# Block 2's mixer: the recurrences, convolutions and head norms laid between the weight tiles of its input projection

## The chip, the cores and the metric

The kernel runs on one core of one Trainium2 chip. The metric is the device time of one execution in microseconds, median of several. TensorE multiplies into eight PSUM banks; VectorE, ScalarE and GpSimd (POOL) do the rest; SyncE (SP) issues most DMAs. Each engine runs its own instructions in order and waits on semaphores.

## The reference

Three blocks in a row work on one sequence of 256 tokens with 1024 channels, all in float32. The change lies in the mixer of the second block; a helper that it edits is used in the first block too. Block 2's mixer is, cut to its operations:

```
z = rmsnorm(x) @ w_in                       # 256 x 3072
a_u, a_gate, b_q, b_f, b_v, b_g, c_b, c_c, c_v = split(z)
y_a = RG-LRU:  u = causal conv(a_u, 4 taps); gates r, i = sigmoid(u @ block-diagonal w)
               a linear recurrence over tokens with decay exp(-8 softplus(lambda) r),
               times gelu(a_gate)
y_b = HGRN2:   f = lower bound + (1 - lower bound) sigmoid(b_f); k = 1 - f; q = silu(b_q)
               gated linear attention with decays f over 6 heads of 64, times silu(b_g)
y_c = short convolution of 3 taps over c_b, c_c, c_v products
x = x + concat(y_a, y_b, y_c, each normed per head of 64 with a gain) @ w_out
```

## The kernel before

**Weights.** A matrix is read in tiles of 1 MB through a ring of three slots (`unit`, `split_act`, `split_dve`). ScalarE rounds a tile into its upper part (`hi`), VectorE subtracts for the lower part (`lo`); three pairs of these exist (NP = 3), so the upper split of tile t waits until TensorE is done with tile t-3. A tile of the input projection (8 x 128 rows, 256 columns) is multiplied in 48 matmuls of 256 columns (`unit_mm`): hi with the upper and the lower part of the activations (L430), lo with the upper part (L435).

**Banks.** `Plan.bank` gives out the eight PSUM banks in turn. Whoever takes a bank waits until the one who had it before, eight takings ago, has been read out.

**Block 2's mixer** is four functions on each engine, each with a `meet` at its end, at which every engine waits for all the others:

1. `block2_in`: norm and transposition, then the twelve tiles of `w_in_2` in their own order; VectorE and ScalarE take turns to copy a finished bank to `z` (24 chunks of 128 channels).
2. `rglru`: a chain of small operations on three columns (L2161 to L2183), three convolutions of four taps (`conv_dve`), six gate products on TensorE (L2131), Tanh on ScalarE, the scan (L2204), Sqrt and Gelu.
3. `hgrn`: the forget gate (Exp, L2253 reciprocal, Ln), SiLU of q, three prefix sums (L752), then the decay of nine levels (`decay_dve`, `decay_act`, `decay_pe`). In level li, VectorE computes the difference E (L762), ScalarE takes Abs and Exp of it (L789, L791), VectorE multiplies it into q and k (L766, L767), TensorE computes the scores of six heads into six banks (L814), and VectorE copies them under a mask into `hS` (L781, L778) one level later. Then TensorE computes the outputs.
4. `mix2_out`: short convolution, squares of all eight chunks, their sums over heads (L671), one Sqrt, one reciprocal over 2048 columns (L680), gain and gate, the parts for TensorE (L390, L397), and the four tiles of the output projection (`rows_pe`, L638).

The order within an engine is the order of the Python calls; nothing plans it. In block 1 `decay_*` runs for GLA with two heads' worth of chunks, and a callable `tick` puts modulation tiles between its levels.

Of the kernel before, what the change touches and what calls it, by code (L numbers as in the profile page):

```python
# [2078 lines left out]
Z_TOK = (12, 13, 14)  # L2079


def block2_in_pe(k, e):
# [2 lines left out]
    first_units_pe(k, e, [k.bank(e, "w_in_2", g) for g in range(2)], u0, ((), ()), "mix2", t["a2_hi"], t["a2_lo"])
    for g in range(2, 12):
        unit_mm(k, e, k.bank(e, "w_in_2", g), u0 + g, t["a2_hi"], t["a2_lo"], [j for j in range(2) if 2 * g + j in Z_TOK])
    meet(k, e, PE_, "z")
# [20 lines left out]

def block2_in_dve(k, e):  # L2110
    t = k.t
# [4 lines left out]
    for g in range(12):  # L2116
        u = k.first["w_in_2"] + g
        split_dve(k, e, u + 3)
        if g % 2 == 0:
            e.wait_ge(*k.used(u))  # L2120
            e.tensor_copy(flat(pair(t["z"], g)), k.got("w_in_2", g)[:, :]).then_inc(*k.DVE(frees=("w_in_2", g)))
    meet(k, e, DVE_, "z")


def rglru_pe(k, e):
    t = k.t
    e.wait_ge(*k.total("rg_in"))
    e.wait_ge(*k.dve("rg", "u"))
    for n, bd, o, _ in RG:
        for c in range(3):  # L2130
            e.matmul(k.bank(e, "rg", o, c)[:, 0:256], t[bd][:, c, :], t["u"][:, c, :]).then_inc(*k.MM("rg", o, c))  # L2131
    meet(k, e, PE_, "rg")
# [1500 lines left out]
```

## Time and profile before

| | |
|---|---|
| median of 3 runs (lowest, highest) | 3101.34 us (3097.02, 3104.08) |
| the profiled execution, its span | 3097.4 us, 3095.5 us |
| TensorE busy | 2799.4 us, 90% |
| VectorE, ScalarE, POOL busy | 46%, 30%, 7% |
| mean granted TensorE clock | 0.938 |

All times in the views are microseconds from the first instruction. The granted clock is in parts of full speed, 1.00 for 2.4 GHz and 0.50 for 1.2 GHz; a value between them is a stretch with both.

### The profile page before, as it was taken

The numbers are of one execution on the slowest core, as the hardware profiler recorded it, in microseconds if no ns is written. First come the engines' busy times: TensorE is split into PE (matmuls) and PEld (weight loads), VectorE is DVE, ScalarE is ACT, GpSimd is POOL, SyncE is SP. The second block draws the span as 40 slices with busy tenths as digits, with TensorE's granted clock in tenths as the row PEclk, the third lists the DMA queues.
The fourth block names the chain that finished last, engine by engine and source line by source line (L and its number), as shares of the span: only waits on it lengthen the run. The fifth ranks groups of instructions, "written<-read, shape, count | busy, mean of one in ns | idle before, by whom it ended". The sixth has DMA issues, their size and how long they took to land. (4 is left out here: it accounts for less than half of the span.)

```text
span 3095.5 us, 42024 instructions
## 1 busy us (share of the span) xinstructions
PE 2799.4 (90%) x17693; PEld 2015.5 (65%) x17693; DVE 1423.2 (46%) x2005; ACT 923.8 (30%) x1217; POOL 222.5 (7%) x160
## 2 busy tenths in 40 slices
...
DMA packets 305130, 713.78 MB, mean 231 GB/s; under 512 B 15723, under 2 KB 214073, under 8 KB 271846
## 3 DMA queue, kind: packets, MB, share of 16 engines
...
## 5 line engine op out<-in xcount | busy, mean ns | idle before, releaser
L369 DVE TENSOR_TENSOR lo<-ring,hi 128x2048 fp32r<-128x2048 f32 x251 | 598.5, 2390 | 298.3 <-ACT hi L360 298.3
L360 ACT ACTIVATE hi<-ring 128x2048 fp32r<-128x2048 f32 x251 | 475.5, 1898 | 191.6 <-PE bank L638 131.4
L1721 PE MATMUL bank<-expert,xg 128*64 128x512 f32 x2304 | 523.6, 599 | 0.0
L430 PE MATMUL bank<-x_hi,hi 128*128 128x256 f32 x1568 | 382.8, 284 | 0.0
L430 PE MATMUL bank<-x_lo,hi 128*128 128x256 f32 x1568 | 380.3, 281 | 0.0
L1721 PEld LDWEIGHTS bank<-expert,xg 128*64 128x64 f32 x2304 | 157.8, 137 | 312.4 <-issue 311.2
L430 PEld LDWEIGHTS bank<-x_hi,hi 128*128 128x128 f32 x1568 | 295.0, 188 | 3.3 <-issue 1.6
L430 PEld LDWEIGHTS bank<-x_lo,hi 128*128 128x128 f32 x1568 | 295.5, 188 | 2.5 <-issue 1.0
L1818 DVE TENSOR_TENSOR acc<-bank,acc 128x512 f32<-128x512 f32 x144 | 89.5, 684 | 407.4 <-PE bank L1808 407.3
L1791 PE MATMUL bank<-expert,aT 128*64 128x512 f32 x1152 | 254.9, 595 | 0.9 <-DMA expert<-in_w_mlp 0.9
L1746 DVE TENSOR_SCALAR sx<-bank 128x256 f32<-128x256 f32 x72 | 30.2, 420 | 395.8 <-PE bank L1732 395.2
L435 PE MATMUL bank<-x_hi,lo 128*128 128x256 f32 x1568 | 204.0, 282 | 0.0
L435 PEld LDWEIGHTS bank<-x_hi,lo 128*128 128x128 f32 x1568 | 194.8, 188 | 0.0
L1791 PEld LDWEIGHTS bank<-expert,aT 128*64 128x64 f32 x1152 | 79.6, 137 | 173.9 <-issue 169.8
L1684 PEld LDWEIGHTS bank<-P,htok 128*128 128x128 f32 x1152 | 137.8, 200 | 26.3 <-issue 26.3
L1700 ACT ACTIVATE xg<-bank 128x512 f32<-128x512 f32 x36 | 21.5, 597 | 444.0 <-PE bank L1684 444.0
L638 PE MATMUL bank<-hi,act_hi 128*128 128x512 f32 x448 | 144.5, 396 | 0.0
L638 PE MATMUL bank<-hi,act_lo 128*128 128x512 f32 x448 | 144.4, 396 | 0.0
L1684 PE MATMUL bank<-P,htok 128*128 128x64 f32 x1152 | 142.3, 284 | 1.1 <-DVE P L1615 1.1
L638 PE MATMUL bank<-lo,act_hi 128*128 128x512 f32 x448 | 119.7, 396 | 0.0
L390 ACT ACTIVATE act_hi<-tmp 128x512 fp32r<-128x512 f32 x56 | 35.4, 633 | 253.9 <-DVE tmp L2687 189.5
L736 POOL MEMSET hS<- 128x2304 f32 x1 | 2.0, 2017 | 1385.2 <-DVE unit L2207 1385.2
...
## 6 DMA issues: line engine op xcount, KB each, us to landing
expert<-in_w_mlp SPq DMA_DIRECT2D x384, 1024.0 KB, 11.5
...
```

Of the source, the lines that this page charges most:

```text
L360: e.activation(k.half("hi", u), k.slot(j), ACT.Copy).then_inc(*k.up("hi_done"))
L369: e.tensor_tensor(k.half("lo", u), k.slot(k.units[u][0]), k.half("hi", u).bitcast(F32), SUB).then_inc(*k.up("lo_done"))
L390: e.activation(hi[:, c:n, :], x[:, c:n, :], ACT.Copy).then_inc(*k.ACT(nm, "hi", c // step))
L430: e.matmul(o, l, r, start=fresh, stop=False, skip_group_check=True)
L435: t = e.matmul(o, l, r, start=False, stop=False, skip_group_check=True)
L638: m = e.matmul(acc[b, h][:, :], x[:, c, b * 128:(b + 1) * 128], w[:, c, h * 512:(h + 1) * 512], start=fresh[b, h], stop=False, skip_group_ ...
L1684: m = e.matmul(bank[:, d * CAP:(d + 1) * CAP], t["htok"][:, b, d * 128:(d + 1) * 128], t[f"P{n % 3}"][:, b, :], start=b == 0, stop=b == 1)
L1700: e.activation(flat(k.t[f"xg{n % 3}"]), k.got("xg", n)[:, :], ACT.Copy).then_inc(*k.ACT("xg", n, frees=("xg", n)))
L1721: i = e.matmul(banks[n][j][h * CAP:(h + 1) * CAP, :], x, W[:, (2 * h + j) * 512:(2 * h + j + 1) * 512], start=c == 0, stop=False, skip_gro ...
L1746: e.tensor_scalar(t[f"sx{j}"], bank[:, 0:512:2], 7.0, None, MIN).then_inc(*k.DVE("gate", "x", n, j))
L1791: q = e.matmul(banks[n][h * CAP:(h + 1) * CAP, :], a, W[:, r, h * 512:(h + 1) * 512], start=i + r == 0, stop=i + r == 4, skip_group_check= ...
L1818: e.tensor_tensor(av, k.got("back", n, b, h)[:, :], av, ADD).then_inc(*k.DVE(frees=("back", n, b, h)))
```

## The change

Block 2's four functions on each engine become one (`block2_pe`, `block2_act`, `block2_dve`) without `meet` between them. The tiles of the input projection come in another order (`Z_ORDER`): first those that hold the forget gate and q, then a_u and the rest. Five are multiplied ahead of the decay; `between_pe`, `between_act` and `between_dve` are called in each level and put one of the other seven tiles, its splits and copies, and pieces of RG-LRU and of the short convolution into levels 0 to 6. ScalarE copies every finished bank to `z`. In `decay_dve` and `decay_act` the difference E of level li+1 is computed and exponentiated in level li. The head norms are split by group and done chunk by chunk: those of RG-LRU and of the short convolution after the last level and ahead of HGRN2's; the output projection takes its tiles in the order 0, 3, 1, 2. POOL clears `hS` and the padded tiles before the projection, not after RG-LRU. Most temporaries share space with `z`, `y2` and `sq2`, so `rgg`, `hg`, `xn2` and `a2o_*` go. The lines taken out of the old functions stand above; of the diff the core:

```diff
     e.wait_ge(*k.dve())
     for li in range(10):
+        if li < 8:
+            h = LEVELS[li + 1]
+            nb, r, v = decay_views(k, nm, n, h)
+            P, E = v(k.t[f"{nm}P{r}"]), v(k.t[f"{nm}E{(li + 1) % 2}"])
+            e.wait_ge(*k.dve())
+            e.tensor_tensor(E, P, P[:, :, h - 1:h].to_broadcast([128, nb, 2 * h]), SUB).then_inc(*k.DVE(nm, "E", li + 1))
         if 0 < li < 9:
             h, i = LEVELS[li], li % 2
             nb, r, v = decay_views(k, nm, n, h)
-            P, E = v(k.t[f"{nm}P{r}"]), v(k.t[f"{nm}E{i}"])
+            E = v(k.t[f"{nm}E{i}"])
             if li >= 2:
                 e.wait_ge(*k.mm(nm, "put", li - 2))
-                e.wait_ge(*k.dve())
-            e.tensor_tensor(E, P, P[:, :, h - 1:h].to_broadcast([128, nb, 2 * h]), SUB).then_inc(*k.DVE(nm, "E", li))
             e.wait_ge(*k.pool(nm, f"qe{i}"))
             e.wait_ge(*k.pool(nm, f"ke{i}"))
             e.wait_ge(*k.act(nm, "E", li))
             e.tensor_tensor(v(k.t[f"{nm}qe{i}"])[:, :, h:2 * h], v(flat(q))[:, :, h:2 * h], E[:, :, h:2 * h], MUL).then_inc(*k.DVE())
             e.tensor_tensor(v(k.t[f"{nm}ke{i}"])[:, :, 0:h], v(flat(kk))[:, :, 0:h], E[:, :, 0:h], MUL).then_inc(*k.DVE(nm, "level", li))
+        if between and li < 9:
+            between(k, e, li)
         if li > 0:
...
-def decay_act(k, e, nm, tick=None):
-    for li in range(10):
-        if 0 < li < 9:
-            E = k.t[f"{nm}E{li % 2}"]
-            e.wait_ge(*k.dve(nm, "E", li))
+def decay_act(k, e, nm, between=None):
+    for li in range(9):
+        if li < 8:
+            E = k.t[f"{nm}E{(li + 1) % 2}"]
+            e.wait_ge(*k.dve(nm, "E", li + 1))
             e.activation(E, E, ACT.Abs).then_inc(*k.ACT())
             e.wait_ge(*k.act())
-            e.activation(E, E, ACT.Exp, scale=-1.0).then_inc(*k.ACT(nm, "E", li))
-        if li > 0 and tick:
-            tick(2 if li - 1 < 6 else 0)
...
+def decay_pe(k, e, nm, q, kk, n, between=None):
     for li, h in enumerate(LEVELS):
-        if tick:
-            tick(2 if li < 6 else 0)
...
+MIX_ORDER = (0, 3, 1, 2)
+def z_unit_pe(k, e, n):
+    t, g = k.t, Z_ORDER[n]
+    unit_mm(k, e, k.bank(e, "w_in_2", n), k.first["w_in_2"] + n, t["a2_hi"], t["a2_lo"], [j for j in range(2) if 2 * g + j in Z_TOK])
+def z_unit_act(k, e, n):
+    u = k.first["w_in_2"] + n
+    split_act(k, e, u + 3)
+    e.wait_ge(*k.used(u))
+    e.activation(flat(pair(k.t["z"], Z_ORDER[n])), k.got("w_in_2", n)[:, :], ACT.Copy).then_inc(*k.ACT("z", n, frees=("w_in_2", n)))
+def z_unit_dve(k, e, n):
+    split_dve(k, e, k.first["w_in_2"] + n + 3)
...
+def head_norm_act(k, e, nm, rt):
+    e.wait_ge(*k.dve(nm, "ms"))
+    e.activation(rt, rt, ACT.Sqrt).then_inc(*k.ACT(nm, "rt"))
+def head_sums_dve(k, e, nm, chunks, rt):
+    for i, c in enumerate(chunks):
+        e.wait_ge(*k.mm(nm, c))
+        e.tensor_scalar(rt[:, i, :], k.got(nm, c)[:, 0:256], EPS, None, ADD).then_inc(*k.DVE(frees=(nm, c)))
+    k.mark("dve_done", nm, "ms")
...
+def block2_pe(k, e):
+    t = k.t
+    first_units_pe(k, e, [k.bank(e, "w_in_2", n) for n in range(2)], k.first["w_in_2"], ((), ()), "mix2", t["a2_hi"], t["a2_lo"])
+    for n in (2, 3, 4):
+        z_unit_pe(k, e, n)
+    e.wait_ge(*k.dve("hg", "in"))
+    decay_pe(k, e, "hg", t["hq"], t["hk"], 3, between_pe)
+    head_norm_pe(k, e, "rgn", (0, 1, 2))
+    head_norm_pe(k, e, "scn", (6, 7))
+    e.wait_ge(*k.act("z", 11))
+    e.wait_ge(*k.dve("hg", "score", 8, 2, 1))
+    for c in range(3):
+        bank = k.bank(e, "hg", "out", c)
+        for par in range(2):
+            decay_out(k, e, t["hS"], 2 * c + par, lambda b, o=par * 64, c=c: t["z"][:, 12 + c, b * 128 + o:b * 128 + o + 64],
+                      bank[par * 64:par * 64 + 64, 0:256], *(("hg", "out", c) if par else ()))
+    head_norm_pe(k, e, "hgn", (3, 4, 5))
+    acc = acc_banks(k, e, "w_out_2")
+    for n, i in enumerate(MIX_ORDER):
+        e.wait_ge(*k.dve("y2", "lo", i))
+        rows_pe(k, e, "w_out_2", acc, k.first["w_out_2"] + n, pair(t["a2_hi"], i), pair(t["a2_lo"], i), n == 0, n == 3)
+    acc_free(k, "w_out_2")
+    meet(k, e, PE_, "mix2")
+def between_pe(k, e, li):
+    t = k.t
+    if li == 2:
+        e.wait_ge(*k.total("rg_in"))
+        e.wait_ge(*k.dve("rg", "u"))
+        for n, bd, o, _ in RG:
+            for c in range(3):
+                e.matmul(k.bank(e, "rg", o, c)[:, 0:256], t[bd][:, c, :], t["u"][:, c, :]).then_inc(*k.MM("rg", o, c))
+    if li < 7:
+        z_unit_pe(k, e, 5 + li)
...
+    e1, e0 = t["rg_sm"][:, 3:6], t["hg_sm"][:, 0:3]
+    split_act(k, e, k.first["w_in_2"] + 3)
+    e.activation(e1, k.V["rg_lambda_2"], ACT.Abs).then_inc(*k.ACT())
+    e.wait_ge(*k.act())
+    e.activation(e1, e1, ACT.Exp, scale=-1.0).then_inc(*k.ACT("rg", "e1"))
+    e.wait_ge(*k.dve("hg", "e0"))
+    e.activation(e0, e0, ACT.Exp).then_inc(*k.ACT("hg", "e0"))
+    z_unit_act(k, e, 0)
+    z_unit_act(k, e, 1)
+    e.wait_ge(*k.act())
+    e.activation(f, f, ACT.Exp, scale=-1.0).then_inc(*k.ACT("hg", "f"))
+    z_unit_act(k, e, 2)
+    e.wait_ge(*k.act())
+    e.wait_ge(*k.dve("mix2", "lo", 3))
+    e.activation(t["hth"], t["hq"], ACT.Tanh, scale=0.5).then_inc(*k.ACT("hg", "q"))
+    e.wait_ge(*k.dve("hg", "k"))
+    e.activation(f, f, ACT.Ln).then_inc(*k.ACT("hg", "ln"))
+    z_unit_act(k, e, 3)
+    z_unit_act(k, e, 4)
+    decay_act(k, e, "hg", between_act)
+    for c in range(3):
+        e.wait_ge(*k.mm("hg", "out", c))
+        e.activation(t["y2"][:, 3 + c, :], k.got("hg", "out", c)[:, 0:256], ACT.Copy).then_inc(*k.ACT(frees=("hg", "out", c)))
+    e.wait_ge(*k.act())
+    e.wait_ge(*k.dve("hg", "g"))
+    e.activation(t["sq2"][:, 3:6, :], t["y2"][:, 3:6, :], ACT.Square).then_inc(*k.ACT("hgn", "sq"))
+    mix_upper_act(k, e, 0)
+    mix_upper_act(k, e, 3)
+    head_norm_act(k, e, "hgn", f)
+    u = k.first["w_out_2"]
+    split_act(k, e, u + 3)
+    mix_upper_act(k, e, 1)
+    mix_upper_act(k, e, 2)
+    for n in (1, 2, 3):
+        split_act(k, e, u + n + 3)
+    meet(k, e, ACT_, "mix2")
...
+def between_act(k, e, li):
+    t, sm = k.t, k.t["rg_sm"]
+    if li < 7:
+        z_unit_act(k, e, 5 + li)
+    if li == 2:
+        e.wait_ge(*k.dve("rg", "hb"))
+        for n, bd, o, hb in RG:
+            for c in range(3):
+                e.wait_ge(*k.mm("rg", o, c))
+                e.activation(t[o][:, c, :], k.got("rg", o, c)[:, 0:256], ACT.Tanh, bias=sm[:, hb + c:hb + c + 1], scale=0.5) \
+                    .then_inc(*k.ACT(*(("rg", o) if c == 2 else ()), frees=("rg", o, c)))
+    elif li == 3:
+        e.wait_ge(*k.dve("rg", "log_a"))
+        e.activation(t["a"], t["r"], ACT.Exp).then_inc(*k.ACT("rg", "a"))
+        e.wait_ge(*k.act())
+        e.activation(t["r"], t["r"], ACT.Tanh).then_inc(*k.ACT("rg", "t"))
+    elif li == 4:
+        e.wait_ge(*k.dve("rg", "b2"))
+        e.activation(t["rb2"], t["rb2"], ACT.Sqrt, scale=-1.0).then_inc(*k.ACT("rg", "beta"))
+        e.activation(t["z"][:, 3:6, :], t["z"][:, 3:6, :], ACT.Gelu_apprx_tanh).then_inc(*k.ACT("rg", "gelu"))
+    elif li == 6:
+        e.activation(t["gth"], t["z"][:, 15:18, :], ACT.Tanh, scale=0.5).then_inc(*k.ACT("hg", "g"))
+        e.wait_ge(*k.dve("sc", "y"))
+        e.activation(t["sq2"][:, 6:8, :], t["y2"][:, 6:8, :], ACT.Square).then_inc(*k.ACT("scn", "sq"))
+        e.wait_ge(*k.dve("rg", "y"))
+        e.activation(t["sq2"][:, 0:3, :], t["y2"][:, 0:3, :], ACT.Square).then_inc(*k.ACT("rgn", "sq"))
+    elif li == 8:
+        head_norm_act(k, e, "rgn", t["z"][:, 0:3, :])
+        head_norm_act(k, e, "scn", t["z"][:, 22:24, :])
...
+def block2_dve(k, e):
+    t, sm, hl, f = k.t, k.t["hg_sm"], k.V["hg_lower_bounds_2"], k.t["z"][:, 9:12, :]
+    e0, lb, om = sm[:, 0:3], sm[:, 3:6], sm[:, 6:9]
+    e.tensor_tensor(e0, hl, hl, SUB).then_inc(*k.DVE("hg", "e0"))
+    split_dve(k, e, k.first["w_in_2"] + 3)
+    rg_decay_dve(k, e)
+    e.wait_ge(*k.act("hg", "e0"))
+    e.reciprocal(lb, e0).then_inc(*k.DVE())
+    e.wait_ge(*k.dve())
+    e.tensor_tensor(e0, e0, lb, MUL).then_inc(*k.DVE())
+    e.wait_ge(*k.dve())
+    e.tensor_tensor(lb, e0, e0, SUB).then_inc(*k.DVE())
+    e.wait_ge(*k.dve())
+    e.tensor_scalar(om, lb, -1.0, 1.0, MUL, ADD).then_inc(*k.DVE())
+    z_unit_dve(k, e, 1)
+    e.wait_ge(*k.act("hg", "f"))
+    e.tensor_scalar(f, f, 1.0, None, ADD).then_inc(*k.DVE())
+    z_unit_dve(k, e, 2)
+    e.wait_ge(*k.dve())
+    e.reciprocal(f, f).then_inc(*k.DVE())
+    e.wait_ge(*k.dve())
+    e.tensor_tensor(f, f, along(om, T), MUL).then_inc(*k.DVE())
+    e.wait_ge(*k.dve())
+    e.tensor_tensor(f, f, along(lb, T), ADD).then_inc(*k.DVE())
+    e.wait_ge(*k.dve())
+    e.tensor_scalar(t["hk"], f, -1.0, 1.0, MUL, ADD).then_inc(*k.DVE("hg", "k"))
+    z_unit_dve(k, e, 3)
+    e.wait_ge(*k.act("hg", "q"))
+    silu_dve(k, e, t["hq"], t["hq"], t["hth"], 0.125)
+    k.mark("dve_done", "hg", "in")
+    z_unit_dve(k, e, 4)
+    e.wait_ge(*k.act("hg", "ln"))
+    e.wait_ge(*k.dve())
+    decay_dve(k, e, "hg", t["hq"], t["hk"], f, 3, t["hS"], between_dve)
+    head_sums_dve(k, e, "rgn", (0, 1, 2), t["z"][:, 0:3, :])
+    head_sums_dve(k, e, "scn", (6, 7), t["z"][:, 22:24, :])
+    head_norm_dve(k, e, "rgn", (0, 1, 2), t["z"][:, 0:3, :])
+    head_norm_dve(k, e, "scn", (6, 7), t["z"][:, 22:24, :])
+    mix_lower_dve(k, e, 0)
+    mix_lower_dve(k, e, 3)
+    head_sums_dve(k, e, "hgn", (3, 4, 5), f)
+    e.wait_ge(*k.act("hgn", "sq"))
+    e.tensor_tensor(t["y2"][:, 3:6, :], t["y2"][:, 3:6, :], t["z"][:, 15:18, :], MUL).then_inc(*k.DVE())
+    u = k.first["w_out_2"]
+    split_dve(k, e, u + 3)
+    head_norm_dve(k, e, "hgn", (3, 4, 5), f)
+    mix_lower_dve(k, e, 1)
+    mix_lower_dve(k, e, 2)
+    for n in (1, 2, 3):
+        split_dve(k, e, u + n + 3)
+    meet(k, e, DVE_, "mix2")
...
+def between_dve(k, e, li):
+    t, V, z, y = k.t, k.V, k.t["z"], k.t["y2"]
+    if li < 7:
+        z_unit_dve(k, e, 5 + li)
+    if li == 0:
+        e.wait_ge(*k.act("z", 4))
+        cw = V["rg_conv_w_2"]
+        for c in range(3):
+            conv_dve(k, e, t["u"][:, c, :], z[:, c, :], [cw[:, j * 3 + c:j * 3 + c + 1] for j in range(4)], V["rg_conv_b_2"][:, c:c + 1])
+        k.mark("dve_done", "rg", "u")
+    elif li == 3:
+        for n, bd, o, _ in RG:
+            e.wait_ge(*k.act("rg", o))
+            e.tensor_scalar(t[o], t[o], 0.5, 0.5, MUL, ADD).then_inc(*k.DVE())
+        e.wait_ge(*k.dve())
+        e.tensor_tensor(t["r"], t["r"], along(t["rg_sm"][:, 21:24], T), MUL).then_inc(*k.DVE("rg", "log_a"))
+        e.tensor_tensor(t["ig"], t["ig"], t["u"], MUL).then_inc(*k.DVE())
+    elif li == 4:
+        e.wait_ge(*k.act("rg", "a"))
+        e.tensor_tensor(t["rb2"], t["a"], t["a"], MUL).then_inc(*k.DVE())
+        e.wait_ge(*k.act("rg", "t"))
+        e.wait_ge(*k.dve())
+        e.scalar_tensor_tensor(t["rb2"], t["rb2"], 1.0, t["r"], ADD, MUL).then_inc(*k.DVE("rg", "b2"))
+    elif li == 5:
+        sw = V["sc_conv_w_2"]
+        e.wait_ge(*k.act("z", 8))
+        e.tensor_tensor(z[:, 20:22, :], z[:, 20:22, :], z[:, 22:24, :], MUL).then_inc(*k.DVE())
+        e.wait_ge(*k.dve())
+        for c in range(2):
+            conv_dve(k, e, y[:, 6 + c, :], z[:, 20 + c, :], [sw[:, j * 2 + c:j * 2 + c + 1] for j in range(3)], None)
+        e.wait_ge(*k.dve())
+        e.tensor_tensor(y[:, 6:8, :], y[:, 6:8, :], z[:, 18:20, :], MUL).then_inc(*k.DVE("sc", "y"))
+    elif li == 6:
+        e.wait_ge(*k.act("rg", "beta"))
+        e.tensor_tensor(t["ig"], t["ig"], t["rb2"], MUL).then_inc(*k.DVE())
+        e.wait_ge(*k.dve())
+        for c in range(3):
+            e.tensor_tensor_scan(t["u"][:, c, :], t["a"][:, c, :], t["ig"][:, c, :], 0.0, MUL, ADD).then_inc(*k.DVE())
+        e.wait_ge(*k.act("rg", "gelu"))
+        e.wait_ge(*k.dve())
+        e.tensor_tensor(y[:, 0:3, :], t["u"], z[:, 3:6, :], MUL).then_inc(*k.DVE("rg", "y"))
+    elif li == 7:
+        e.wait_ge(*k.act("hg", "g"))
+        silu_dve(k, e, z[:, 15:18, :], z[:, 15:18, :], t["gth"], 1.0)
+        k.mark("dve_done", "hg", "g")
...
+        z = k.sb("z", [128, 24, 256], F32, c3)
+        k.sb("a2_hi", [128, KC, 256], F32R, c3), k.sb("a2_lo", [128, KC, 256], F32R, c3)
+        k.sb("rg_sm", [128, 24], F32, c3), k.sb("hg_sm", [128, 16], F32, c3)
+        k.sb("hk", [128, 3, 256], F32, c3)
+        k.sb("hS", [128, 6, 3, 128], F32, c3)
+        lay_decay(k, "hg", 3, c3)
+        k.t["hq"], k.t["rb2"] = z[:, 6:9, :], z[:, 0:3, :]
+        k.t["hth"] = k.t["u"] = k.t["sq2"][:, 0:3, :]
+        k.t["r"] = k.t["gth"] = k.t["sq2"][:, 3:6, :]
+        k.t["a"], k.t["ig"] = k.t["y2"][:, 0:3, :], k.t["y2"][:, 3:6, :]
+    for g in Z_ORDER:
+        k.unit("w_in_2", wview(A["w_in_2"][0])[:, :, g * 256:(g + 1) * 256], 8, 256)
+    for i in MIX_ORDER:
+        k.unit("w_out_2", wview(A["w_out_2"][0])[:, 2 * i:2 * i + 2, :], 2, DM)
```

`u + 3` in `z_unit_act` means that the upper split for tile n+2 is issued ahead of the copy of tile n. `rg_decay_dve` holds the small operations that were L2161 to L2183.

## Rows read from the trace of the kernel before

**Rows 1.** Table of stretches (start:end, length, busy by engine, granted clock, DMA share, GB/s)
```profile
1417.70:1477.80 60.10, 59.48 (x504) 59.28 (x503) 26.98 (x16) 22.16 (x16) 0.00 (x0) 1.00 0.55 178
1477.80:1519.70 41.90, 4.46 (x12) 3.39 (x12) 28.43 (x62) 16.88 (x23) 5.15 (x5) 0.57 0.05 21
1519.70:1574.20 54.50, 26.88 (x205) 24.27 (x205) 38.18 (x81) 14.32 (x17) 0.00 (x0) 0.50 0.00 1
1574.20:1616.50 42.30, 10.83 (x44) 6.53 (x44) 28.80 (x23) 6.66 (x6) 0.00 (x0) 0.58 0.00 0
1616.50:1640.70 24.20, 24.15 (x96) 19.11 (x96) 10.77 (x7) 8.18 (x6) 0.00 (x0) 0.93 0.42 132
```

**Rows 2.** Waits of TensorE from 1519.7 to 1640: total, times, longest
```profile
PE bank L814 <- DVE hq L718: 25.1, 1, 25.1
```

**Rows 3.** Timeline of ScalarE, block 2: start, length, operation, idle before
```profile
1477.22 0.60 ACT L2106 ACTIVATE z<-bank 128x512 f32<-128x512 f32 x1 [3.79 <-PE bank L435]
...
1505.19 1.28 ACT L2227 ACT_TABLE_LOAD   x1 [2.28 <-DVE hg_sm L2241]
...
1550.97 0.84 ACT L791 ACTIVATE hgE<-hgE 128x768 f32<-128x768 f32 x1
...
1624.00 1.92 ACT L360 ACTIVATE hi<-ring 128x2048 fp32r<-128x2048 f32 x1 [5.07 <-PE bank L638]
```

**Rows 4.** Timeline of VectorE, block 2
```profile
1508.08 4.95 DVE L2253 RECIPROCAL z<-z 128x768 f32<-128x768 f32 x1
...
1519.74 5.05 DVE L752 TENSOR_TENSOR_SCAN hgP<-early,hg 128x768 f32<-128x768 f32 x3
...
1549.10 0.96 DVE L762 TENSOR_TENSOR hgE<-hgP 128x768 f32<-128x768 f32 x1
...
1552.42 0.55 DVE L767 TENSOR_TENSOR hgke<-hk,hgE 128x384 f32<-128x384 f32 x1
1552.89 2.09 DVE L781 COPY_PREDICATED hS<-im,bank 128x256 f32<-128x256 int32 x6
...
1572.83 1.27 DVE L778 COPY hS<-bank 128x128 f32<-128x128 f32 x6
...
1596.31 12.95 DVE L680 RECIPROCAL xn<-xn 128x2048 f32<-128x2048 f32 x1 [1.98 <-ACT xn L665]
...
1618.96 2.29 DVE L369 TENSOR_TENSOR lo<-ring,hi 128x2048 fp32r<-128x2048 f32 x1 [0.86 <-ACT hi L360]
```

**Rows 5.** Table of stretches, VectorE alone: convolution, RG-LRU, SiLU, short convolution
```profile
1484.30:1490.10 5.80, 5.42 (x13) 0.50 0.00 0
1493.70:1504.80 11.10, 8.64 (x11) 0.65 0.00 0
1579.10:1580.90 1.80, 1.53 (x4) 1.00 0.00 0
1580.90:1585.10 4.20, 3.93 (x8) 0.67 0.00 0
```

**Rows 6.** Timeline of TensorE: first tile, pitch of tiles, gates, scores of a level
```profile
1404.49 3.75 PE L606 MATMUL bank<-a_hi,hi 128*128 128x256 f32 x16 [11.59 <-ACT hi L360]
...
1421.29 2.04 PE L435 MATMUL bank<-a_hi,lo 128*128 128x256 f32 x16
...
1426.92 2.04 PE L435 MATMUL bank<-a_hi,lo 128*128 128x256 f32 x16
...
1490.29 4.46 PE L2131 MATMUL bank<-u,BD 128*128 128x256 f32 x12 [13.11 <-DVE u L729]
...
1541.07 3.09 PE L814 MATMUL bank<-hgqe,hgke 64*128 64x128 f32 x24 [2.89 <-DVE hgke L767]
```

**Rows 7.** Table of stretches, block 1's decay
```profile
148.00:152.00 4.00, 2.88 (x22) 1.69 (x22) 0.76 (x2) 1.03 (x3) 0.00 (x0) 0.59 1.10 353
```

**Rows 8.** Timeline of TensorE, block 1's last two decay levels
```profile
168.35 1.51 PE L814 MATMUL bank<-glaqe,glake 64*128 64x128 f32 x16 [3.09 <-DVE glake L767]
172.70 1.22 PE L810 MATMUL bank<-glaqe,glake 64*128 64x128 f32 x8 [2.85 <-DVE glake L767]
```

More of the change, by code:

```diff
@@ L745, in decay_views, with decay_dve @@
     return W // (2 * h), r, v
-def decay_dve(k, e, nm, q, kk, g, n, S, tick=None):
+def decay_dve(k, e, nm, q, kk, g, n, S, between=None):
     W = n * 256
@@ L2076 @@
 RG = (("rg_w_r_2", "BD0", "r", 15), ("rg_w_i_2", "BD1", "ig", 18))
+Z_ORDER = (4, 5, 3, 0, 1, 2, 9, 10, 11, 8, 7, 6)
 Z_TOK = (12, 13, 14)
-def block2_in_pe(k, e):
-    t, u0 = k.t, k.first["w_in_2"]
-    turn_rows_pe(k, e, "mix2")
[L2085 to L2088, printed above, removed]
@@ new lines, in head_norm_pe @@
+def head_norm_pe(k, e, nm, chunks):
+    e.wait_ge(*k.act(nm, "sq"))
+    for c in chunks:
+        e.matmul(k.bank(e, nm, c)[:, 0:256], k.cc("bones"), k.t["sq2"][:, c, :]).then_inc(*k.MM(nm, c))
+def head_norm_act(k, e, nm, rt):
[6 more added lines that the diff above has]
+    k.mark("dve_done", nm, "ms")
@@ new lines, in head_norm_dve, with mix_upper_act @@
+def head_norm_dve(k, e, nm, chunks, rt):
+    t, gain = k.t, k.V["mix_out_gain_2"]
+    e.wait_ge(*k.act(nm, "rt"))
+    for i, c in enumerate(chunks):
+        e.reciprocal(rt[:, i, :], rt[:, i, :]).then_inc(*k.DVE())
+        e.wait_ge(*k.dve())
+        e.scalar_tensor_tensor(t["y2"][:, c, :], t["y2"][:, c, :], gain[:, c:c + 1], rt[:, i, :], MUL, MUL).then_inc(*k.DVE("y2", c))
+def mix_upper_act(k, e, i):
+    e.wait_ge(*k.dve("y2", 2 * i))
+    e.wait_ge(*k.dve("y2", 2 * i + 1))
+    e.activation(pair(k.t["a2_hi"], i), pair(k.t["y2"], i), ACT.Copy).then_inc(*k.ACT("y2", "hi", i))
@@ L2115, in block2_in_dve @@
         e.memset(t[f"BD{i}"], 0.0).then_inc(*(k.DVE("BD") if i else k.DVE()))
[L2116 to L2132, printed above, removed]
@@ L2205, in rglru_dve @@
-    e.wait_ge(*k.act("rg", "gelu"))
-    e.wait_ge(*k.dve())
-    e.tensor_tensor(t["y2"][:, 0:3, :], t["u"], t["rgg"], MUL).then_inc(*k.DVE())
-    meet(k, e, DVE_, "rg")
-def hgrn_pe(k, e):
-    t = k.t
-    e.wait_ge(*k.dve("hg", "in"))
-    decay_pe(k, e, "hg", t["hq"], t["hk"], 3)
-    e.wait_ge(*k.dve("hg", "score", 8, 2, 1))
-    for c in range(3):
-        bank = k.bank(e, "hg", "out", c)
-        for par in range(2):
-            decay_out(k, e, t["hS"], 2 * c + par, lambda b, o=par * 64, c=c: t["z"][:, 12 + c, b * 128 + o:b * 128 + o + 64],
-                      bank[par * 64:par * 64 + 64, 0:256], *(("hg", "out", c) if par else ()))
-    meet(k, e, PE_, "hg")
@@ L2224, in hgrn_act @@
-def hgrn_act(k, e):
-    t, f, e0 = k.t, k.t["z"][:, 9:12, :], k.t["hg_sm"][:, 0:3]
-    e.wait_ge(*k.dve("hg", "e0"))
-    e.activation(e0, e0, ACT.Exp).then_inc(*k.ACT("hg", "e0"))
-    e.activation(f, f, ACT.Exp, scale=-1.0).then_inc(*k.ACT("hg", "f"))
-    e.wait_ge(*k.dve("hg", "f"))
-    e.activation(t["hg"], f, ACT.Ln).then_inc(*k.ACT("hg", "ln"))
-    e.activation(t["hq"], t["z"][:, 6:9, :], ACT.Tanh, scale=0.5).then_inc(*k.ACT("hg", "q"))
-    decay_act(k, e, "hg")
-    e.wait_ge(*k.mm("hg", "put", 8))
-    e.activation(t["hq"], t["z"][:, 15:18, :], ACT.Tanh, scale=0.5).then_inc(*k.ACT("hg", "g"))
-    meet(k, e, ACT_, "hg")
```

180 lines of the change are left out of this document (21 added, 159 removed).

## The prediction

> **What bounds the kernel now.** I read the table of stretches first, because the change touches one stage of 3095.5 us and the page's averages hide it. [rows 1] cut block 2's mixer at the places where its parts meet. From 1417.7 us, when the second weight tile of the input projection is done, ten tiles keep TensorE busy for 59.5 of 60.1 us. Then the three functions behind it run one after another, each behind a `meet`: RG-LRU and the preparation of HGRN2 (41.9 us, TensorE busy 4.5), the nine decay levels (54.5 us, TensorE busy 26.9 at a granted clock of 0.50), HGRN2's output with the short convolution and the head norms (42.3 us, busy 10.8), and the output projection (24.2 us, busy throughout). So for 138.7 us no weight tile is multiplied. VectorE is busy for 95.4 of these, and the rest is handed back and forth: [rows 2] show TensorE waiting 25.1 us for VectorE's `hq` alone. In this stage the chain is VectorE with ScalarE in the gaps; TensorE sets the time only in the two projections. From 1417.7 to the end of the output projection at 1640.7 it takes 223.0 us. The ends of this stretch are the same in both kernels: ahead of it the norm and the first two tiles, behind it a `meet` and the load of `p_tok`.
>
> **What is added, removed, moved.** The work stays nearly the same. Seven of the twelve weight tiles go between the decay levels (tile 5+li ahead of the scores of level li), with their splits, the convolutions and RG-LRU on VectorE and ScalarE. Three `meet`s go. ScalarE copies all twelve banks (0.60 us each, VectorE's six go). What matters is what each engine now has queued ahead of what another waits for, so I follow the queues from 1417.7 with durations from rows.
>
> (a) To the end of the prefix sums. ScalarE: copy of tile 1, Exp of the forget gate, upper split of tile 4 (0.6 + 0.8 + 1.9, [rows 3]), with the tail of the split ahead 3.8. VectorE: lower split 2.3, reciprocal 4.95, two products of 0.96, `hk` 0.6 [rows 4]: 9.8. Ln and the next upper split 2.9. VectorE: lower split 2.3, SiLU 1.5 [rows 5], lower split 2.3, three scans 5.05: 11.2. Together 27.7; tiles 2, 3 and 4 (5.63 each, the pitch in [rows 6]) lie beside it and end at 1434.6. The small RG-LRU chain of some 25 operations on three columns moves to 1411, where VectorE waited for tiles: nothing.
>
> (b) Level 0: difference E1 0.96, then on ScalarE Abs 0.84, a table load 1.28 (Ln was last), Exp 0.84, and only behind these the upper split 1.9 that VectorE's lower split 2.3 waits for; then the first convolution 5.8 [rows 5]. 13.9 with hand-overs.
>
> (c) Levels 1 to 6. The next level's E is issued first, and ScalarE's in-order queue holds Abs and Exp of it ahead of the upper split of tile 7+li. So VectorE, which has 0.96 + 1.1 + 2.3 + 2.1 = 6.5 of work (E, two products, split, six masked copies), is held to 0.96 + 0.84 + 0.84 + 1.9 + 2.3 + 2.1 + 0.15 = 9.1. The two products run inside the wait. TensorE has a tile and 24 score matmuls, 5.63 + 3.09 [rows 6] = 8.7 with the scores at the low clock: hidden by 0.4, and the tile is needed two levels later. 6 x 9.1 = 54.6.
>
> (d) What lies on top in these levels. Level 2 is the one new wait. PSUM has eight banks in turn, and each `bank` waits for the one taken eight places before. A level takes seven (a tile, six scores), and level 2 takes six more for the RG-LRU gates, ahead of tile 7. The third to sixth of these wait for VectorE's copies of level 1's scores, the last thing VectorE does in level 2. From that moment: four or more gate matmuls 1.3 (twelve took 4.46, [rows 6]), tile 7 5.9, its copy 0.6, six Tanh 2.8, and only then Abs, Exp and upper split 3.6 for level 3: 14.2, where an ordinary level needs 4.6. So VectorE sits idle some 12 us in level 3 and 9.6 is lost. RG-LRU's VectorE part (11.1 us with waits, 8.6 busy, [rows 5]) spreads: 3.05 in level 3, 1.95 in 4, 3.9 in 6. Level 5 takes the short convolution, 4.1, and 1.4 for ScalarE, late after Sqrt, Gelu and the table load back to Exp. Sum 24.0.
>
> (e) Levels 7 and 8 and the last copies, with no split left: 0.96 + 1.1 + 1.5 (SiLU of the gate) + 2.1; 1.1 + 2.1; 1.3: 10.1.
>
> (f) The tail. Before, one reciprocal of 2048 columns took 12.95 [rows 4], with two products of 2.3 and four lower splits, all ahead of the first output tile. Now the norms of chunks 0 to 2 and 6, 7 alone stand ahead of it: five sums 2.1, five reciprocals of 256 columns (an eighth of 12.95, 1.62) with a product of 0.48 (conv row: twelve in 5.8), 10.6, one lower 0.65, hand-overs 0.2: 13.6. HGRN2's three norms (6.3) and a split (4.2 with its wait) run beside the first two output tiles; pair 1 is ready some 14 us after they began and they take 12.8 of the 24.2, so the third tile may be 1 us late, which I leave to the range. The output projection is unchanged, 24.2 [rows 1].
>
> Sum: 27.7 + 13.9 + 54.6 + 24.0 + 10.1 + 13.6 + 24.2 = 168.1 against 223.0: 55 less in block 2.
>
> **Block 1's decay.** The same three functions serve GLA, and there too each level's E is now issued a level early, so Abs and Exp no longer lie between E and the products. While weight tiles stand between its levels the DMA engines are full (share 1.10, [rows 7]) and TensorE waits for tiles; I put these levels at nothing. Behind them TensorE waited 3.09 and 2.85 us for the products of levels 7 and 8 [rows 8], about half of each for Abs and Exp of a narrower E than block 2's. Between 0 and 5.9; I take 3, half of both waits. With it the gain is 58: the profiled execution took 3097.4 us with a span of 3095.5, so it gives 3039; it lay 3.9 under the median 3101.34, and the forecast is the median less 58, 3043.
>
> **What I put at nothing.** POOL's memsets (5.15 us busy, [rows 1]) start some 120 us earlier, past two `meet`s, under the norm of block 2; they are first needed in level 1. If that cover went, 5 us. The ring's loads have two levels (18 us) of lead. The DMAs of the gate weights stay where they were. The split of tile t waits for tile t-3, long done. A hand-over costs 0.03 to 0.2 us in the rows; double everywhere, the sum loses 3.
>
> **A table switch.** [rows 3] show ACT_TABLE_LOAD 1.28 us and the function starting at once behind it; that is the price above, for two switches that I place on the chain (levels 0 and 5). The Trainium skill (ScalarE: Activation LUTs, What ACT_TABLE_LOAD costs) adds a drain of about 1.38 us to each switch. By it the two would cost 2.8 us more and the gain would be 55; this trace shows no such drain.
>
> **The rivals.**
> 1. The array stays at the low clock through the levels. Before, it was granted 0.50 in all of them [rows 1], with 3 us pauses; in block 1, where weight tiles of another kind stood between levels, the grant fell to 0.59 with TensorE busy 2.88 of 4 us [rows 7]. At 1.2 GHz a tile takes double, 11.3 (sixteen matmuls took 3.75 in [rows 6], against 2.04 at 2.4 GHz), and a level 14.4, over the 9.1. From 1438, seven such levels, the gates 4.5 and the Tanhs 3 end at 1546; the last scores and copies 10 later, some 10 us behind the forecast: 3053. Against it: TensorE is busy some nine tenths of a level, not half. The Trainium skill (TensorE: Matmul & The Clock Gate, HAM oscillation) says that pauses between bursts bring the low clock back and each burst then starts cold; by that rule this rival holds.
> 2. The levels run at VectorE's own 6.5 and the wait of level 2 is short, 25 us less: 3018. Nothing in the queues allows the first; if only the wait of level 2 is short, 3033.
> 3. Half the gain is lost to something that rows don't show (slower splits beside busy TensorE, a later landing): 3072.
> 4. It is slower. A level becomes a serial loop: tile (cold 11.3), scores 3.1, and only then VectorE's 9.1, because the tile's bank waits for the last masked copy and ScalarE's queue for the tile's copy. 23.5 a level, 14.4 over mine, seven times: 101 lost, 43 net: 3144. It decides from 17 us a level. Against it: the split in a level waits for the tile before, which is done.
>
> **Chances.** The forecast 0.70 (3033 to 3053: the hand-overs, the clock partly low); rival 1 0.12; rival 2 0.08; rival 3 0.06; rival 4 0.04. The range 3030 to 3063 leaves out rivals 3, 4 and the far end of 2. A change of 0.2% (6 us) is about what a measurement tells from none. Faster by more than that: 0.95; within: 0.01; slower: 0.04.
>
> **What would show it.** Right: the first scores at 1445 or so; levels of about 9 us, VectorE waiting some 2.6 us for the upper split in each; one wait of 12 us in level 3 behind the Tanhs; the last masked copies near 1547; the first output matmul near 1561 and the last near 1585; a granted clock near 1.00 between. Wrong: tiles of 11 us, no long wait in level 3, levels over 12 us, or a third output tile that waits more than 3 us for `a2_lo`.

## The result and the profile after

The changed kernel takes 3043.06 us (median of 4 runs, 3040.05 to 3045.72); beside it the kernel before took 3099.91. The ratio is 0.9818, 95% interval 0.9802 to 0.9834: 1.8% faster, 56.9 us by the medians. A second set of 5 runs gave 3041.5 (3040.88 to 3044.55) against 3099.46, ratio 0.9813 (0.98 to 0.9826), 58.0 us. The forecast was 3043.

The profiled execution took 3044.36 us, its span 3042.6 at a mean granted clock of 0.948. Its table of stretches, cut at the ends of the forecast's parts, answers [rows 1]: end of the scans, start of E in level 1, of level 3 and of level 4, E of level 7, last masked copy, first and last matmul of the output projection.

```profile
1415.60:1442.60 27.00, 24.27 (x217) 23.94 (x217) 22.31 (x14) 11.40 (x11) 0.00 (x0) 1.00 0.48 155
1442.60:1456.40 13.80, 6.20 (x55) 5.88 (x51) 8.55 (x14) 5.26 (x5) 0.00 (x0) 0.81 0.25 80
1456.40:1474.20 17.80, 7.63 (x32) 6.10 (x33) 12.40 (x21) 7.45 (x7) 0.00 (x0) 0.60 0.26 68
1474.20:1496.60 22.40, 19.84 (x146) 18.62 (x146) 9.10 (x15) 8.45 (x13) 0.00 (x0) 0.88 0.23 88
1496.60:1535.10 38.50, 31.48 (x241) 29.95 (x241) 28.17 (x45) 19.78 (x20) 0.00 (x0) 0.85 0.23 83
1535.10:1545.00 9.90, 8.37 (x50) 7.08 (x48) 9.71 (x25) 2.97 (x3) 0.00 (x0) 0.50 0.00 0
1545.00:1559.80 14.80, 6.57 (x50) 5.08 (x49) 13.55 (x16) 4.70 (x8) 0.00 (x0) 0.85 0.00 1
1559.80:1585.30 25.50, 24.63 (x96) 19.21 (x96) 19.38 (x17) 9.45 (x8) 0.00 (x0) 0.92 0.38 123
```

The stretch that took 223.0 us before takes 169.7. TensorE is busy 129.0 of it. Its waits, which answer [rows 2], are now many short ones, and the longest stands ahead of level 1's scores (total, times, longest):

```profile
PE bank L822 <- DVE hS L789: 13.9, 6, 4.1
PE bank L822 <- DVE hgke L772: 10.3, 2, 9.6
```

VectorE's timeline shows what sets the levels now. L761 is E of the next level, L369 the lower split of a weight tile, L789 the masked copies of the level before:

```profile
1456.44 0.96 DVE L761 TENSOR_TENSOR hgE<-hgP 128x768 f32<-128x768 f32 x1
1457.32 0.55 DVE L771 TENSOR_TENSOR hgqe<-z,hgE 128x384 f32<-128x384 f32 x1
1457.79 0.55 DVE L772 TENSOR_TENSOR hgke<-hk,hgE 128x384 f32<-128x384 f32 x1
1460.99 2.29 DVE L369 TENSOR_TENSOR lo<-ring,hi 128x2048 fp32r<-128x2048 f32 x1 [2.65 <-ACT hi L360]
1463.20 2.09 DVE L789 COPY_PREDICATED hS<-im,bank 128x256 f32<-128x256 int32 x6
1465.32 0.96 DVE L761 TENSOR_TENSOR hgE<-hgP 128x768 f32<-128x768 f32 x1
...
1489.29 2.29 DVE L369 TENSOR_TENSOR lo<-ring,hi 128x2048 fp32r<-128x2048 f32 x1 [13.19 <-ACT hi L360]
...
1513.79 2.29 DVE L369 TENSOR_TENSOR lo<-ring,hi 128x2048 fp32r<-128x2048 f32 x1 [4.39 <-ACT hi L360]
...
1548.08 1.75 DVE L2133 RECIPROCAL z<-z 128x256 f32<-128x256 f32 x1
```

From one E to the next is 8.88 us in an ordinary level (1456.44 to 1465.32), and 2.65 of them VectorE is idle because the upper split of the tile isn't there. In level 3 the same wait is 13.19 us. ScalarE's and TensorE's timelines show why:

```profile
1457.44 0.84 ACT L797 ACTIVATE hgE<-hgE 128x768 f32<-128x768 f32 x1 [8.51 <-DVE hgE L761]
1458.31 0.84 ACT L799 ACTIVATE hgE<-hgE 128x768 f32<-128x768 f32 x1
1459.06 1.89 ACT L360 ACTIVATE hi<-ring 128x2048 fp32r<-128x2048 f32 x1
...
1483.06 0.60 ACT L2103 ACTIVATE z<-bank 128x512 f32<-128x512 f32 x1 [13.23 <-PE bank L435]
1483.56 1.20 ACT L2244 ACTIVATE x<-bank,rg_sm 128x256 f32<-128x256 f32 x3
1484.62 1.22 ACT L2244 ACTIVATE unit<-bank,rg_sm 128x256 f32<-128x256 f32 x3
1485.69 0.89 ACT L797 ACTIVATE hgE<-hgE 128x768 f32<-128x768 f32 x1
```

```profile
1463.69 2.93 PE L822 MATMUL bank<-hgqe,hgke 64*128 64x128 f32 x20 [4.07 <-DVE hS L789]
1466.55 1.92 PE L2182 MATMUL bank<-x,BD 128*128 128x256 f32 x4
1472.57 3.78 PE L2182 MATMUL bank<-x,BD 128*128 128x256 f32 x8 [4.10 <-DVE hS L789]
```

Four gate matmuls run; the other eight wait 4.10 us for banks that VectorE's masked copies (from 1472.08) give back. Behind them tile 7 runs, its copy starts on ScalarE at 1483.06, six Tanhs follow, and only then Abs and Exp of E4 and the upper split for which VectorE waits.

### The profile page after: what moved, and what is told of

The parts are those of the page before. It is cut to its first block and busy times, and to the rows that moved or that the text cites. A ratio compares the mean times of both kernels' runs of the same rounds, so it can differ in the third digit from the quotient of the medians.

```text
span 3042.6 us, 42056 instructions
## 1 busy us (share of the span) xinstructions
PE 2805.2 (92%) x17701; PEld 2020.3 (66%) x17701; DVE 1419.2 (47%) x2013; ACT 927.5 (30%) x1230; POOL 220.2 (7%) x160
## 5 line engine op out<-in xcount | busy, mean ns | idle before, releaser
L369 DVE TENSOR_TENSOR lo<-ring,hi 128x2048 fp32r<-128x2048 f32 x251 | 601.9, 2404 | 298.8 <-ACT hi L360 298.8
L638 PE MATMUL bank<-hi,act_hi 128*128 128x512 f32 x448 | 144.6, 397 | 0.0
L638 PE MATMUL bank<-hi,act_lo 128*128 128x512 f32 x448 | 144.3, 396 | 0.0
L638 PE MATMUL bank<-lo,act_hi 128*128 128x512 f32 x448 | 119.6, 396 | 0.0
L638 PEld LDWEIGHTS bank<-lo,act_hi 128*128 128x128 f32 x448 | 84.4, 188 | 20.5
```

Of the source, the lines that this page charges most:

```text
L369: e.tensor_tensor(k.half("lo", u), k.slot(k.units[u][0]), k.half("hi", u).bitcast(F32), SUB).then_inc(*k.up("lo_done"))
L638: m = e.matmul(acc[b, h][:, :], x[:, c, b * 128:(b + 1) * 128], w[:, c, h * 512:(h + 1) * 512], start=fresh[b, h], stop=False, skip_group_ ...
```

## The experiments

All are edits of the changed kernel, of order or place alone. The ratio is to the kernel before in the same set of runs.

**Upper split first.** In each level ScalarE splits the tile ahead of Abs and Exp, not behind them (`ahead` calls `split_act` for it, and the later call in `z_unit_act` finds it done).

```diff
-def decay_act(k, e, nm, between=None):
+def decay_act(k, e, nm, between=None, ahead=None):
     for li in range(9):
+        if ahead and li < 7:
+            ahead(k, e, li)
         if li < 8:
```

> In each level ScalarE makes the upper split ahead of Abs and Exp of the next E, not behind. If the levels are set by VectorE waiting for ScalarE's queue, each wait of 2.65 us for the upper split goes, about 2.7 us in each of seven levels: 19 to 21 us less, 3023; the wait in level 3 stays, some 9 to 11 us. If TensorE sets the levels (8.7 us of tile and scores), nothing or at most 0.4 us a level is gained: 3040 to 3043.

Measured: 3020.73 us, 0.9746 (0.9729 to 0.9762), 22.3 under the changed kernel. VectorE's timeline of this kernel:

```profile
1450.51 0.96 DVE L761 TENSOR_TENSOR hgE<-hgP 128x768 f32<-128x768 f32 x1
1452.32 2.28 DVE L369 TENSOR_TENSOR lo<-ring,hi 128x2048 fp32r<-128x2048 f32 x1
1456.64 0.96 DVE L761 TENSOR_TENSOR hgE<-hgP 128x768 f32<-128x768 f32 x1
...
1473.42 2.29 DVE L369 TENSOR_TENSOR lo<-ring,hi 128x2048 fp32r<-128x2048 f32 x1 [8.75 <-ACT hi L360]
```

An ordinary level is now 6.13 us (1450.51 to 1456.64), and the splits don't wait. So the 8.88 were VectorE held by ScalarE's queue. Had TensorE set them, with a tile and 24 score matmuls, this order would have changed next to nothing.

**The tile ahead of the gates.** In level 2 `z_unit_pe` is issued ahead of the gate products, so that tile 7 runs while banks are waited for.

```diff
     t = k.t
+    if li < 7:
+        z_unit_pe(k, e, 5 + li)
     if li == 2:
...
-    if li < 7:
-        z_unit_pe(k, e, 5 + li)
```

> In level 2 tile 7 is multiplied ahead of the six RG-LRU gate products instead of behind them. If the bank wait is what costs level 3 its 13 us (the gates can't start before VectorE's last copies of level 1, and the tile stands behind them), VectorE's longest wait for an upper split falls from 13.2 us to about 3, and the time by 8 to 9 us, to about 3035. If instead TensorE's own work sets these levels (tile, gates and scores one after another at the low clock), the order does not matter: 3043, within 2.

Measured: 3037.34 us, 0.9791 (0.9775 to 0.9808): 5.7 less by the medians, 7.0 by the spans. The wait in level 3 fell to 4.08 us, and the level from 22.35 to 13.25 us, E to E:

```profile
1478.12 0.96 DVE L761 TENSOR_TENSOR hgE<-hgP 128x768 f32<-128x768 f32 x1
1484.10 2.29 DVE L369 TENSOR_TENSOR lo<-ring,hi 128x2048 fp32r<-128x2048 f32 x1 [4.08 <-ACT hi L360]
...
1491.37 0.96 DVE L761 TENSOR_TENSOR hgE<-hgP 128x768 f32<-128x768 f32 x1
```

That is 9.1 us in the level, as the waiting chain has it. From E of level 1 to the first output matmul it is 108.07 us, against 117.29 in the first profile of the changed kernel: 9.2 less. The span shows only 7.0 because this execution came to that E 3.9 us later (1446.57 against 1442.65), ahead of the edit's place, and got 2.1 us back at the wait for `p_tok` (5.12 against 7.18).

**Both together.**

> Tile 7 ahead of the gate products and ScalarE's upper split ahead of Abs and Exp, together. The two waits are separate parts of one chain of VectorE, so most of both gains should add: by the queues 26 us less than the changed kernel, 3016. If TensorE becomes the bound once VectorE's levels are shorter (a tile and its scores take 8.7 us with the scores at the low clock), nothing more than the upper split's gain is left: 3021.

Measured: 3015.52 us, 0.973 (0.9714 to 0.9746). The wait in level 3 is 5.01 us here, not 8.75 as with the upper split alone. The two overlap: with the upper split ahead, part of the wait of level 3 is covered already.

**Block 2's E back in its own level.**

```diff
-        if li < 8:
-            h = LEVELS[li + 1]
+        lag = 1 - (nm == "hg")
+        if 0 < li + lag < 9:
+            h = LEVELS[li + lag]
```

and the same in `decay_act`.

> In block 2's decay E of a level is computed in that level again, as before the change; all else stays. By the queues nothing is lost: the upper split stands behind Abs and Exp either way and VectorE's lower split behind the upper one, so a level stays at 9 us; only the wait moves, from ahead of the lower split to ahead of the products: 3043, within 2. If computing E a level early is what brings the levels' gain, each level loses Abs and Exp, 1.7 us in eight levels: 3057.

Measured: 3042.53 us, 0.9807 (0.9791 to 0.9824), against the changed kernel's 3043.06: no difference. Between tiles the early E is worth nothing in this order. VectorE's waits in the levels, first this kernel, then the changed one:

```profile
DVE hgqe L772 <- ACT hgE L801: 28.6, 8, 11.4
DVE lo L369 <- ACT hi L360: 4.1, 6, 0.7
```

```profile
DVE lo L369 <- ACT hi L360: 33.0, 7, 13.2
```

28.6 + 4.1 is 32.7, against 33.0: E, Abs, Exp and upper split are one chain of ScalarE, and it only changes at which instruction VectorE waits for it.

**All twelve tiles ahead of the decay.** The splits and copies go with them; the pieces of RG-LRU and of the short convolution stay in the levels.

```diff
-    for n in (2, 3, 4):
+    for n in range(2, 12):
         z_unit_pe(k, e, n)
```

and the same for the two other engines, with the calls in `between_*` taken out.

> All twelve tiles are multiplied ahead of the decay, nothing of them between the levels; the pieces of RG-LRU and the short convolution stay in the levels, as do the early E and the split head norms. If the overlap with the tiles is where the gain comes from, seven tiles of 5.7 us come back onto the chain: about 3083. By the queues the levels lose the split hand-over (about 4.2 us each in place of 9.1) and the bank wait, and TensorE is full while the tiles run: the decay begins some 30 us later and ends some 8 to 10 earlier: about 3034.

Measured: 3029.28 us, 0.9768 (0.9752 to 0.9784). That is 13.8 less than with the tiles laid between the levels. Then the same with E in its own level:

> All tiles ahead of the decay and E of a level computed in that level again. With no upper split between Abs, Exp and VectorE's next work, the early E should now be worth what it was not worth between tiles: a level goes from about 4.2 to about 6.0 us, some 17 us on the kernel with all tiles ahead: 3046. If the early E is worth nothing anywhere, 3029.

Measured: 3050.31 us, 0.9847 (0.9831 to 0.9864): 21.0 more by the medians, 18.5 by the spans. Without splits between them the levels run at VectorE's pace, and there the early E pays. In the trace of this kernel, VectorE waits for E in each of the eight levels, 17.6 us in all; in the one with the early E it has no such wait:

```profile
1492.81 0.96 DVE L762 TENSOR_TENSOR hgE<-hgP 128x768 f32<-128x768 f32 x1
1495.65 0.56 DVE L772 TENSOR_TENSOR hgqe<-z,hgE 128x384 f32<-128x384 f32 x1 [1.88 <-ACT hgE L801]
```

**The first output tile late.** TensorE waits for all four pairs of `a2_lo` before the output projection.

```diff
     acc = acc_banks(k, e, "w_out_2")
+    e.wait_ge(*k.dve("y2", "lo", MIX_ORDER[3]))
```

> The changed kernel, but the first tile of the output projection waits until the parts of all eight chunks are ready. This takes away what the split head norms bring by an early start: the first output tile begins some 14 us later, and the time rises by 13 to 14 us, to about 3057. If the tail is bound by the output tiles' splits or by VectorE's total work, not by when the first parts are ready, within 3 us of 3043.

Measured: 3057.07 us, 0.9867 (0.9851 to 0.9884): 14.0 more. TensorE's timeline:

```profile
1574.88 1.19 PE L638 MATMUL bank<-hi,a_hi 128*128 128x512 f32 x2 [21.94 <-DVE a_lo L2146]
```

It waits 21.94 us where the changed kernel waits 7.03. HGRN2's norms are really hidden by the first two output tiles, and the early start that the split of the norms allows is worth 14 of the 57 us.

**`p_tok` with a space of its own.** `p_tok` is what the stage behind the mixer transposes first. It is loaded at that stage's start, since it shares its space. Here it has its own and its load is issued at the start of block 2.

```diff
     split_act(k, e, k.first["w_in_2"] + 3)
+    e.dma_start(t["p_tok"], k.A["p_2"][0, 0].rearrange("(b p) n -> p b n", p=128)).then_inc(*k.up("p_in", by=16))
```

> The changed kernel, but p_tok has a place of its own and its load is issued at the start of block 2. In the changed kernel it lands 7 us after it is asked for, behind three weight tiles of the ring, against 4.7 us before the change, and TensorE waits for it. If the wait is on the chain, it goes with its issue: 6 to 7 us less, 3036. If the norm's sums behind it are the chain, nothing.

Measured: 3039.48 us, 0.9807 (0.979 to 0.9823). The wait is gone: from the first output matmul to the first of L638 that reads `p_hi` it is 29.56 us (1559.26 to 1588.82), against 36.95 and 34.53 in the two profiles of the changed kernel. By the medians only 3.6 or 2.0 remain. Some 1.5 us are lost again 190 us later. The table of stretches at the first matmuls that read `f2a_hi`, of this kernel and of the changed kernel's second profile:

```profile
1782.50:1787.50 5.00, 4.97 (x15) 3.97 (x16) 3.28 (x3) 1.05 (x1) 0.00 (x0) 0.67 0.37 135
```

```profile
1786.40:1791.40 5.00, 4.93 (x21) 4.01 (x22) 3.88 (x5) 1.10 (x1) 0.00 (x0) 1.00 0.38 141
```

The grant is 0.67 where it was 1.00, and 15 matmuls run in place of 21. From there to the end of TensorE's next long wait it is 40.82 us in this kernel and 39.36 in the other. The same shows in the next kernel (0.66, 40.92). But it shows too in the kernel with block 2's E back in its own level, which doesn't have this edit (0.66, 40.89):

```profile
1790.20:1795.20 5.00, 5.00 (x15) 4.01 (x16) 3.25 (x3) 1.01 (x1) 0.00 (x0) 0.66 0.37 140
```

In the ten other profiles without the edit the grant there is 1.00. So an early `p_tok` isn't needed for the drop, and that it brings it on is not shown.

**All three.** The upper split first, the tile ahead of the gates, and `p_tok` early.

> Three edits together: the tile ahead of the gate products in level 2, the upper split ahead of Abs and Exp in every level, and p_tok with a space of its own, loaded at the start of block 2. The first two gave 3015.5 together, the third alone took 3.6 from the median and some 7 from the stretch that it acts on. If they add: 3010, from 3008 to 3013. If the load's gain was the difference between two executions: 3015.

Measured: 3014.26 us (3013.33 to 3016.47), 0.9724 (0.971 to 0.9737). The expectation that they add was 3010 and is missed; the other one, 3015, is nearer. Against the 3015.52 without the load the intervals overlap, so the load's own worth here is not shown. By its median it is the fastest kernel of this study, 85 us under the one before.

**Block 1's decay in its old order.** The edit is that of "E back in its own level", for GLA. It was made because I had come to doubt that term: in the first profile after, block 1's levels were no shorter.

> Block 1's decay in its old order (E of a level computed and exponentiated in that level), block 2 as changed. The theory: block 1's levels are bound by the ring's loads, so the earlier E is worth nothing there, and the time is that of the changed kernel, 3043, within 1.5. The prediction's term (half of the waits of levels 7 and 8 saved) has it 3 longer: 3046.

> The changed kernel once more, beside the two below and on the same chip, as what they are compared with. Both theories expect 3043, within 3.

Measured: 3044.49 us (3042.16 to 3051.5), 0.9824 (0.9811 to 0.9838), against 3041.5 and 0.9813 (0.98 to 0.9826). The medians lie 3.0 apart, but the intervals overlap, so I go by the traces. TensorE's timeline at levels 7 and 8, which answers [rows 8]: this kernel, then the second profile of the changed one.

```profile
163.84 2.16 PE L824 MATMUL bank<-glaqe,glake 64*128 64x128 f32 x32
169.08 1.26 PE L824 MATMUL bank<-glaqe,glake 64*128 64x128 f32 x16 [3.09 <-DVE glake L773]
173.49 1.27 PE L820 MATMUL bank<-glaqe,glake 64*128 64x128 f32 x8 [3.15 <-DVE glake L773]
```

```profile
125.37 3.64 PE L1064 MATMUL bank<-ring,sc 128*32 128x256 f32 x32 [3.99 <-DVE g L1305]
...
165.00 2.16 PE L822 MATMUL bank<-glaqe,glake 64*128 64x128 f32 x32
168.69 1.26 PE L822 MATMUL bank<-glaqe,glake 64*128 64x128 f32 x16 [1.54 <-DVE glake L772]
170.81 1.27 PE L818 MATMUL bank<-glaqe,glake 64*128 64x128 f32 x8 [0.86 <-DVE glake L772]
```

The two waits take 6.24 us in the old order and 2.40 in the new. From level 5's scores to those of level 8 (163.84 to 173.49, and 165.00 to 170.81) it is 9.65 us here and 9.60 in the kernel before. In nine of the eleven profiles with the new order it is 5.8, in the other two 6.4. So the early E takes 3.2 to 3.8 us off these levels in every profile.

The length of the whole decay hides that. From its first modulation matmul (125.37 in the second view above) to level 8's scores it is 48.13 us before and 49.14 here. In the eleven profiles with the new order it is 44.05 to 50.20, with the median at 45.4. The longest is that of all tiles ahead, the shortest that of `p_tok` alone, and block 1 runs the same code in both. The table of stretches shows this part in the two:

```profile
123.58:173.78 50.20, 42.53 (x357) 26.84 (x357) 24.89 (x56) 16.62 (x33) 0.00 (x0) 0.66 0.76 252
```

```profile
123.42:167.47 44.05, 35.51 (x356) 22.21 (x356) 24.69 (x56) 16.60 (x33) 0.00 (x0) 0.81 0.86 278
```

The same matmuls are busy 7.0 us longer at a grant of 0.66 than at 0.81, while the waits for ring loads are about the same (2.75 and 2.50 us). The first profile after was one of the long ones, 48.55 us at a grant of 0.70; the second had 45.44 at 0.80. The doubt fell: it rested on one execution.

## Why the prediction was right

The verdict, the size and the mechanism all held. That the median came out at 3043 to the tenth is luck: block 2 took 1.6 us more than its sum, and the median of the kernel before was 3101.34 when the forecast was made and 3099.91 beside the result. The parts of the forecast's sum against the table of stretches of the first profile after:

| part | forecast | measured |
|---|---|---|
| (a) to the end of the scans | 27.7 | 27.0 |
| (b) level 0 | 13.9 | 13.8 |
| (c), (d) levels 1 to 6 with what lies on top | 78.6 | 78.7 |
| (e) levels 7, 8, last copies | 10.1 | 9.9 |
| (f) to the first output tile | 13.6 | 14.8 |
| (g) output projection | 24.2 | 25.5 |
| sum | 168.1 | 169.7 |

- **(b), the table switch.** ScalarE's timeline has ACT_TABLE_LOAD at 1444.51 for 1.28 us and the Exp at 1445.80, again with nothing between. The drain that the Trainium skill (ScalarE: Activation LUTs, What ACT_TABLE_LOAD costs) adds isn't seen here either: the Abs ahead ended at 1444.49.
- **(c), the ordinary level.** Forecast 9.1, measured 8.88, with 2.65 us of waiting where 2.6 was forecast. The reason is shown, not only the size: with the upper split first the level is 6.13, and with E back in its own level the time stays.
- **(d), the wait of level 3.** Forecast 12, measured 13.19. From the end of the last masked copies the chain was put at 14.2 us and took 15.1 (1474.17 to 1489.26). The gates and tile 7 took 8.9 where 7.2 was forecast, because the array came out of a pause at the low clock (grant 0.60 up to there), and the Tanhs took 2.1 for 2.8. The tile moved ahead of the gates took the wait to 4.08, so the place of the cause is shown.
- **(f).** Five reciprocals of 256 columns took 1.75 each, not an eighth of the 12.95 in [rows 4] (1.62), and two sums waited 0.43 us each for TensorE. Together that is 1.5, a little over the miss of 1.2.
- **(g).** The third tile waited 0.64 us for `a_lo`; about 1 was left to the range.
- **Block 1.** Forecast 3 less. From level 5's scores to level 8's it is 3.2 to 3.8 less in every profile. The length of the whole decay says 3.2 (median 45.4 against 48.6, the mean of the two of the old order), but it scatters by more. The medians say 3.0, with intervals that overlap.
- **Behind the mixer** nothing was forecast to change. In the first profile after, `p_tok` was waited for 7.18 us against 4.74 before. In the nine other profiles of changed kernels in which TensorE waits for it, with the second of the changed kernel among them (4.75), it is 4.75 to 5.36. So it was that execution, and the forecast stands.

In spans, the two profiles of the changed kernel lie 52.9 and 55.0 us under the one before (3042.6 and 3040.5 against 3095.5). The second is 53.7 from the stretch (from 1415.7 to the end of the output projection at 1585.0), 2.0 from an earlier start, and 0.7 back. The medians say 57 and 58; the profiled execution of before (3097.4) lay 2.5 and 2.1 under the medians of before in the two sets, and those of after 1.3 over and 0.8 over theirs.

**The rivals.** Rival 1 named the clock rightly in part. The grant was 0.60 in levels 1 and 2, where TensorE paused 4 to 10 us at a time. The rule of the Trainium skill (TensorE: Matmul & The Clock Gate, HAM oscillation), that bursts start cold behind long pauses, agrees with these two levels. In levels 7 and 8 the grant was 0.50 though TensorE was busy 8.37 of 9.9 us, most of it with score matmuls. But the rival's time was wrong, since the levels weren't TensorE's. What the low clock cost on the chain is, as an estimate, the 1.7 us in (d) and 0.2 in (g), where the first output tile took 7.40 us against 7.19 before. My "granted clock near 1.00 between" was wrong: 0.85 to 0.88 in levels 3 to 6. Rival 2 was refused because "nothing in the queues allows" levels at VectorE's own pace. With the queues changed for it (upper split first, the tile ahead of the gates) both its halves came: 3015.52 where it had 3018. Rival 3's unseen loss isn't there. Rival 4 decided from 17 us a level; the level was 8.88.

**Where the gain comes from.** That the tiles lie between the levels is not what gives it, in this order: with all tiles ahead of the levels the kernel is 13.8 us faster, some 71 under the one before. Of these 71, 21.0 by the medians (18.5 by the spans) are the early E, which pays only where no splits lie between, and 14.0 the early start of the output projection, if it is worth there what it is worth in the changed kernel. The other 36 or so are what is left: the pieces of RG-LRU and the short convolution inside the levels, the rest of block 2's new order, and block 1's 3; they were not tried one by one. With the upper split first, the levels do cover the tiles: 3020.73 against 3029.28.
